# Grouped attention with split values and the probabilities of four query blocks in one matmul

## The chip, the cores and the metric

One core of one Trainium2 chip runs one program. The time is the device time of one execution in microseconds (us), the median of several. The engines are TensorE (PE; its weight loads are listed as PEld), VectorE (DVE), ScalarE (ACT), GpSimd (POOL) and SyncE (SP), which issues the DMAs.

## The reference, cut to what matters

The program is a chain of two transformer blocks. The change touches one stage of the second: attention of 512 latent tokens, 8 query heads in 2 groups, over 768 keys (512 latent and 256 context ones), without a mask.

```python
q, k, v = jnp.split(h @ w_qkv, [nq, nq + nk], axis=-1)    # 8 q heads, 2 k, 2 v, width 128
q = _rmsnorm(q..., q_gain); k = _rmsnorm(k..., k_gain)    # and rotary on the latent ones
keys = jnp.concatenate([kl, kc], axis=1)                  # 768
s = jnp.einsum('bqkgd,bskd->bkgqs', q, k).astype(jnp.float32) * (ATTN_HEAD_DIM ** -0.5)
p = jax.nn.softmax(s, axis=-1).astype(v.dtype)
o = jnp.einsum('bkgqs,bskd->bqkgd', p, v)
y_lat = o @ w_o
```

All is float32. The kernel forms nearly all products from two parts (`hi`, the rounded value in the format fp32r, and `lo`, the rest): `three()` makes one product of three fp32r matmuls, hi by hi, hi by lo and lo by hi.

## The kernel before

Every engine has its own program, written out by hand, and the engines wait for each other through counting semaphores; what stands behind a waiting instruction on its engine waits too.

Projection. `project(g, ...)` runs for g = 0 to 3: keys and values of the context, keys and values of the latents, queries 0 to 3, queries 4 to 7. Each g is four chunks of weights (`b + 4g` to `b + 4g + 3`) and uses the four PSUM banks `4 * (g % 2)` and up, so g = 2 writes over the banks of g = 0, and g = 3 over those of g = 1. The weights go through four slots: ACT makes `w_hi` (`split_hi`, L1909) once a slot is free, DVE then makes `w_lo` (`split_lo`, L1929). Values are turned by PE from `vT_att` into banks 2 and 3 (g = 0) or 4 and 5 (g = 1) in `value_turns`, and ACT copies them to `v_att` (L2303, semaphore `vt_s`). PE waits for that copy (`vt_s`) before `project(2)` and `project(3)`.

Attention. A unit is a head u; it has four query blocks c of 128 tokens. A step is (u, c), 32 steps in all. In a step PE turns the 6 x 128 probabilities of the block (`turn_`, L1124, two groups of three), makes the scores of the block two steps later (`scores`, three fp32r matmuls of 512 and three of 256 columns, L1045 to L1047), and multiplies the turned probabilities with the values (`values`, L1135): 6 matmuls of plain f32 with 128 columns, each listed as two records. DVE takes the scores out with scale and maximum (`maxima`, L2699), ACT makes the exponentials (`exps`, L2018), and the turned probabilities leave PSUM half on DVE (`take`, L2709), half on ACT (L2026). `finish` (L2715, L2725) divides by the sum on DVE, with queries on partitions.

Output. `project_out` first turns the eight head outputs (32 transposes, L1254), ACT and DVE split them (L2100, L2843), and then `three()` multiplies them with the chunks of `attn_w_o`.

The last queries are prepared between the scores of the first two blocks and the first `turn_` (`last_queries`, handed in as `beside`).

Of the kernel before, what the change touches and what calls it, by code (L numbers as in the profile page):

```python
# [28 lines left out]
P = 128  # L29
# [152 lines left out]
def build(nc, w, tables, out):  # L182
    ctx = ExitStack()
    with ctx:
# [96 lines left out]
        class Work:  # L281


            def __init__(self, tag, at, size, start, width):
                self.sm = arena("scores" + tag, [P, 2, width], F32, at, size, start)
                self.pT = arena("probs_T" + tag, [P, 2, 512], F32, at + 8 * width, size, start)

# [28 lines left out]
        v_att = arena("v_att", [P, 6, 2 * P], F32, 22528)  # L316
        vT_att = arena("vT_att", [P, 2, SEQ], F32, 28672)
        o_att = arena("o_att", [P, 4, D_MODEL], F32, 32768)
        zeros = arena("zeros", [P, SEQ + CTX], F32, 49152)

        work_att = Work("_att", 52224, ARENA_SIZE, None, 3072)
# [95 lines left out]
        rl_s = sem("rl_s")  # L417
        spread_s = sem("spread_s")
# [132 lines left out]
        def attention_plan(heads, blocks, **what):  # L551

            full = blocks == "full"
            units = len(heads)
            at = Phase("attention", units=units, heads=heads, full=full, per_t=8 if full else 4, **what)
            at.tab_in = tab_s.planned
            at.s0, at.sm0 = s_s.plan(4 * units), sm_s.plan(4 * units)
            at.p0, at.t0, at.ptd0, at.pta0 = p_s.plan(4 * units), t_s.plan(at.per_t * units), ptd_s.plan(at.per_t // 2 * units), pta_s.plan(at.per_t // 2 * units)
            at.pv0, at.o0, at.step0 = pv_s.plan(at.per_t * units), o_s.plan(units), dve_step.plan(sum(3 if h["gate"] is not None else 1 for h in heads))
            return at  # L560
# [36 lines left out]
        def out_plan(ph, tile, turned):  # L597

            ph.o_tile = tile
            if turned:  # L600
                ph.tr0 = tr_s.plan(KT)
            ph.oh0, ph.ol0 = a_hi_s.plan(KT), a_lo_s.plan(KT)
            ph.d0 = down_s.plan(KT - 1)
            x_done.plan(KT)
            bank_half[0] ^= 4

        def even_phase():
# [37 lines left out]
            out_plan(ph, o_tile, False)  # L645
            return ph

        def mla_phase():
# [22 lines left out]
            out_plan(ph, o_tile, False)  # L671
# [24 lines left out]
        def attn_phase():  # L696
# [14 lines left out]
            for i in range(2):  # L711
                splits.append((k_att[:, i, :], k_att_hi[:, i, :], k_att_lo[:, i, :]))
                for u in range(4):
                    h = 4 * i + u
                    splits.append((q_att[:, h, :], q_att_hi[:, h, :], q_att_lo[:, h, :]))
                    heads.append(dict(q=splits[-1][1:], k=splits[5 * i][1:], v=lambda kb, i=i: v_att[:, kb, i * P:i * P + P],
                                      out=o_att[:, :, h * P:h * P + P], gate=None, need=ph.qk0 + len(splits),
                                      scale=lambda c, h=h: q_rstd[:, 4 * h + c:4 * h + c + 1]))
            ph.first_splits = splits[0:4]
            ph.att = attention_plan(heads, "full", work=work_att, mask=zeros[:, :], dim=P, later=[[x] for x in splits[4:]])  # L720
            ph.att.nrm0, ph.att.rstd_in = ph.nrm0, ph.head_rstd0 + 6
            out_plan(ph, lambda k: (a_hi[:, k, :], a_lo[:, k, :]), True)
# [317 lines left out]
        def _(pe):  # L1040
# [46 lines left out]
            def attention(at, beside=None):  # L1087

                wk, full, per_t, D = at.work, at.full, at.per_t, at.dim
                ring = 2 if full else 4  # L1090
                units_t = [(c, range(3 * h, 3 * h + 3)) for c in range(4) for h in range(2)] if full else \
                    [(c, range(c + 1)) for c in range(4)]

                def scores(u, c):
                    head = at.heads[u]
                    if c == 0 and head["need"] is not None:
                        pe.wait_ge(qk_lo_s.sem, head["need"])
                    if c == 0 and head.get("rope") is not None:
                        pe.wait_ge(rope_in[4].sem, 16 * 4)
                        pe.wait_ge(head["rope"].sem, 16 * 4)  # L1100
                    if 4 * u + c >= ring:

                        pe.wait_ge(sm_s.sem, at.sm0 + 4 * u + c - ring + 1)
                    parts = [(0, 512, 2 * (c % 2)), (512, 768, 2 * (c % 2) + 1)] if full else [(0, (c + 1) * P, c)]
# [2507 lines left out]
```

## Time and profile before

| | us |
|---|---|
| median of 3 runs | 3199.8 (3199.59 to 3200.89) |
| the profiled execution | 3202.26 |
| its span, first to last instruction | 3200.4 |
| PE busy in the span | 3131.4 (98%) |
| stretch from the first `turn_` to the first output matmul | 2675.86 to 2778.51 |

The execution's time is 1.86 us more than its span. Positions in the trace are given in us from the span's start.

### The profile page before, as it was taken

Reading aid. Unit: us, or ns where it says so; the run is one execution under the profiler, and the core shown is the slowest. Engines: PE = TensorE matmul, PEld = TensorE weight load, DVE = VectorE, ACT = ScalarE, POOL = GpSimd, SP = SyncE. Lnnn points to the kernel's source line nnn. Section 1 sums busy time; section 2 is a strip of 40 time slices with the busy share of each in tenths; the row PEclk is TensorE's granted clock in tenths of the full one; section 3 lists DMA queues with packets and bytes.
Section 4 is the critical chain, followed back from the end, with each engine's and each line's share of the span. In section 5 each row is a group of like instructions: output and inputs, shape, how many; then the busy total and the mean of one; then the engine's idle time right before and its main releaser. Section 6 shows DMA issues by size and latency. Waiting matters only on the chain.

```text
span 3200.4 us, 43004 instructions
## 1 busy us (share of the span) xinstructions
PE 3131.4 (98%) x15821; PEld 2601.3 (81%) x15821; DVE 1969.8 (62%) x2773; ACT 1258.4 (39%) x1920; POOL 177.8 (6%) x176
## 2 busy tenths in 40 slices
PE   8999999899999999999999999999999999999999
PEld 6888877678888888886788888989888887878887
DVE  6764557866755676457765554897555465565543
ACT  3222323752222422236642233765334354453332
POOL 1000011100000000000120000332000001000000
PEclk9999999999999999999999999999999999999999
DMA  6543342025532454332145433554332220123332
GB/s 182 169 139 102 107 123 66 1 78 159 164 116 94 126 169 145 99 98 66 52 137 168 135 102 106 165 153 144 92 104 93 91 98 7 33 73 97 100 100 71
DMA packets 388599, 346.11 MB, mean 108 GB/s; under 512 B 12512, under 2 KB 340637, under 8 KB 388477
## 3 DMA queue, kind: packets, MB, share of 16 engines
q1 hardware_dynamic: 388477, 344.49, 35.8%
q8 instruction: 76, 1.25, 0.2%
q14 instruction: 46, 0.38, 0.0%
HBM read 338.22 MB, written 2.10 MB: 106 GB/s over the span
## 4 chain that ended last, share of the span: by engine, by line
PE 87%; DVE 8%; ACT 3%; issue 1%; SPq 1%; DMA 0%; POOL 0%; ACTq 0%; DVEq 0%; POOLq 0%
PE ps L1045 26%; PE ps L1047 26%; PE ps L1046 26%; DVE w_lo L1929 2%; PE ps L1135 1%; ACT scores_even L2061 1%; PE ps L1193 1%; PE ps L1208 1%; PE ps L1228 1%; SPq L936 1%; PE ps L1124 1%; DVE scores_even L2773 0%; PE ps L1787 0%; PE ps L1788 0%; PE ps L1786 0%
## 5 line engine op out<-in xcount | busy, mean ns | idle before, releaser
L1045 PE MATMUL ps<-a_hi,w_hi 128*128 128x512 f32 (+1 forms) x2920 | 1106.0, 379 | 23.7 <-DVE w_lo L1929 8.4
L1046 PE MATMUL ps<-a_lo,w_hi 128*128 128x512 f32 (+1 forms) x2920 | 1098.9, 376 | 0.0
L1047 PE MATMUL ps<-a_hi,w_lo 128*128 128x512 f32 (+1 forms) x2920 | 1098.4, 376 | 0.0
L1929 DVE TENSOR_TENSOR w_lo<-w_raw,w_hi 128x1024 fp32r<-128x1024 f32 (+1 forms) x526 | 642.1, 1244 | 178.9 <-ACT w_hi L1909 176.1
L1909 ACT ACTIVATE w_hi<-w_raw 128x1024 fp32r<-128x1024 f32 (+1 forms) x526 | 543.6, 1046 | 362.6 <-PE ps L1047 302.4
L1045 PEld LDWEIGHTS ps<-a_hi,w_hi 128*128 128x128 f32 x2920 | 551.9, 189 | 129.1 <-issue 20.4
L1046 PEld LDWEIGHTS ps<-a_lo,w_hi 128*128 128x128 f32 x2920 | 552.2, 189 | 101.1 <-issue 2.0
L1047 PEld LDWEIGHTS ps<-a_hi,w_lo 128*128 128x128 f32 x2920 | 551.9, 189 | 100.6
L1045 PE MATMUL ps<-hs_hi,w_hi 128*128 128x512 f32 x1008 | 392.7, 390 | 1.0 <-DVE hs_lo L3274 1.0
L1047 PE MATMUL ps<-hs_hi,w_lo 128*128 128x512 f32 x1008 | 392.2, 389 | 0.0
L1046 PE MATMUL ps<-hs_lo,w_hi 128*128 128x512 f32 x1008 | 392.2, 389 | 0.0
L2396 ACT ACTIVATE t<-t 128x512 f32<-128x512 f32 x88 | 55.6, 632 | 518.9 <-DVE t L3251 518.9
L3253 DVE TENSOR_TENSOR t<-ps,rstd 128x512 f32<-128x512 f32 x88 | 60.8, 691 | 293.8 <-PE ps L1047 293.8
L2410 ACT ACTIVATE hs_hi<-hid 128x512 fp32r (+1 forms) x126 | 79.5, 631 | 406.0 <-PE ps L1047 406.0
L1045 PEld LDWEIGHTS ps<-hs_hi,w_hi 128*128 128x128 f32 x1008 | 189.2, 188 | 40.7 <-DVE hs_lo L3274 1.5
L1047 PEld LDWEIGHTS ps<-hs_hi,w_lo 128*128 128x128 f32 x1008 | 189.2, 188 | 39.2
L1046 PEld LDWEIGHTS ps<-hs_lo,w_hi 128*128 128x128 f32 x1008 | 189.2, 188 | 39.1
L3274 DVE TENSOR_TENSOR hs_lo<-hid,hs_hi 128x512 fp32r<-128x512 f32 x106 | 73.3, 691 | 218.2 <-ACT hs_hi L2410 218.2
L3239 DVE SCALAR_TENSOR_TENSOR t<-ps,cols,t 128x511 f32<-128x511 f32 x88 | 66.0, 750 | 188.0 <-ACT t L2389 187.9
L3296 DVE SCALAR_TENSOR_TENSOR ada_acc<-ada_raw,cond,ada_acc 128x1024 f32<-128x1024 f32 x147 | 180.5, 1279 | 0.0
L2389 ACT ACTIVATE t<-ps,cols 128x512 f32<-128x512 f32 x88 | 68.6, 779 | 206.5 <-PE ps L1047 206.5
L3266 DVE TENSOR_TENSOR hid<-t,t 128x512 f32 x108 | 74.8, 693 | 17.9 <-DVE t L3253 9.6
(394 smaller groups left out, 3105.2 us busy)
## 6 DMA issues: line engine op xcount, KB each, us to landing
w_raw<-in_ffn_w_up SPq DMA_DIRECT2D x220, 512.0 KB, 4.7
w_raw<-in_ffn_w_down SPq DMA_DIRECT2D x154, 512.0 KB, 3.5
ada_raw<-in_ada_w SPq DMA_DIRECT2D x96, 512.0 KB, 3.9
w_raw<-in_ffn_w_gate SPq DMA_DIRECT2D x88, 512.0 KB, 4.9
w_raw<-in_ev_w_in SPq DMA_DIRECT2D x20, 512.0 KB, 4.4
w_raw<-in_attn_w_qkv SPq DMA_DIRECT2D x12, 512.0 KB, 3.9
w_raw<-in_mla_w_out SPq DMA_DIRECT2D x8, 512.0 KB, 3.6
w_raw<-in_attn_w_o SPq DMA_DIRECT2D x8, 512.0 KB, 3.5
```

The source lines that it names most:

```text
L1045: mm(dst, hi, rhi, start=start, stop=False)
L1046: mm(dst, hi, rlo, start=False, stop=False)
L1047: return mm(dst, lo, rhi, start=False, stop=stop)
L1909: nc.scalar.activation(w_hi[:, s, 0:width], w_raw[:, s, 0:width], ACT.Copy).then_inc(hi_made.sem, 1)
L1929: nc.vector.tensor_tensor(w_lo[:, s, 0:width], w_raw[:, s, 0:width], w_hi[:, s, 0:width].bitcast(F32), ALU.subtract).then_inc(lo_made.sem, 1)
L2389: do(t[:, 0:T], ps[:, ph.half + 2 * (f % 2) + side, 0:T], ACT.Identity, scale=conv_column(1, side, f, it), bias=conv_column(3, side, f, it ...
L2410: do(dst, src, ACT.Copy).then_inc(h_hi_s.sem, 1)
L3239: v.scalar_tensor_tensor(t[:, 1:T], src[:, 0:T - 1], conv_column(0, side, f, it), t[:, 1:T], ALU.mult, ALU.add).then_inc(mid.sem, 1)
L3253: v.tensor_tensor(t2[:, 0:T], ps[:, f2 + 1, 0:T], rstd[:, 0:T], ALU.mult).then_inc(up_s.sem, 1)
L3266: v.tensor_tensor(hid[:, bass.ds(it * 2 + f, 1), 0:T], t1[:, 0:T].unsqueeze(1), t2[:, 0:T].unsqueeze(1), ALU.mult).then_inc(h_s.sem, 1)
L3274: v.tensor_tensor(lo, src, hi.bitcast(F32), ALU.subtract).then_inc(h_lo_s.sem, 1)
L3296: last = v.scalar_tensor_tensor(acc, ada_raw[:, u, :], cond[:, c, bass.ds(it, 1)], acc, ALU.mult, ALU.add)
```

## The change

Values are kept in two parts, `v_att_hi` (ACT) and `v_att_lo` (DVE, new `value_rests`), and PE waits for the second part (`vl_s`) before `project(2)` and `project(3)`. In attention the values are the stationary operand. For each of the six key blocks j of a head, PE turns the probabilities of all four query blocks into one bank (four transposes), ACT rounds them to `pT_att_hi`, DVE makes `pT_att_lo` after that, and `three()` adds v x p with 512 columns. The head's output then has its features on partitions. The inverses of the sums are spread over partitions by four more transposes (`inverse_rows`), ACT takes them to `o_att`, DVE multiplies (`scaled`), ACT and DVE split the result (`out_hi`, `out_lo`) into the places where the head's queries lay. `project_out` has no transposes any more, and takes the output columns in the order 4 to 7, 0 to 3 for its first chunk.

```diff
-                    pe.wait_ge(vt_s.sem, ph.vt0 + 2)
+                    pe.wait_ge(vl_s.sem, ph.vl0 + 2)
...
-                    pe.wait_ge(vt_s.sem, ph.vt0 + 4)
+                    pe.wait_ge(vl_s.sem, ph.vl0 + 4)
...
-                    for i, kb in enumerate(kbs):
-                        last = mm(ps[:, 6 + u % 2, c * D:(c + 1) * D], wk.pT[:, j % 2, i * P:(i + 1) * P],
-                                  at.heads[u]["v"](kb), start=(kb == 0), stop=(kb == (5 if full else c)))
-                    last.then_inc(pv_s.sem, 1)
...
+                    slot = (6 * u + j) % 2
+                    three(ps[:, 6 + u % 2, :], *at.heads[u]["v"](j), pT_att_hi[:, slot, :], pT_att_lo[:, slot, :], j == 0, j == 5)\
+                        .then_inc(pv_s.sem, 1)
+
+                scores(0, 0)
+                scores(0, 1)
+                beside()
+                scores(0, 2)
+                scores(0, 3)
                 for u in range(at.units):
...
+                    for j in range(7):
+                        if j < 6:
+                            turn_(u, j)
+                        else:
+                            inverse_rows(u)
+                        if j < 4 and u + 1 < at.units:
+                            scores(u + 1, j)
+                        if j:
+                            values(u, j - 1)
...
+                for c in range(4):
                     exps(0, c)
                 for u in range(at.units):
...
+                    for j in range(6):
+                        turned_hi(u, j)
+                        if 1 <= j <= 4 and u + 1 < at.units:
                             exps(u + 1, j - 1)
...
+                        if j == 2 and u:
+                            out_hi(u - 1)
+                        if j == 4 and u < len(at.later):
+                            if u != 1:
+                                act.wait_ge(nrm_s.sem, at.nrm0 + 6 + max(0, u - 1))
+                            qk_hi(at.later[u])
+                    rows_taken(u)
+                out_hi(at.units - 1)
...
+                def turned_lo(u, j):
+                    n = 6 * u + j
+                    dve.wait_ge(pta_s.sem, at.pta0 + 7 * u + j + 1)
+                    v.tensor_tensor(pT_att_lo[:, n % 2, :], ps[:, 4 + (7 * u + j) % 2, :], pT_att_hi[:, n % 2, :].bitcast(F32),
+                                    ALU.subtract).then_inc(ptd_s.sem, 1)
...
+                    inverse(u)
+                    for j in range(6):
+                        turned_lo(u, j)
+                        if j < 4 and u + 1 < at.units:
                             maxima(u + 1, j)
...
+                        if j == 1 and u:
+                            scaled(u - 1)
+                        if j == 2 and u < 4:
+                            roped(u)
+                        if j == 3 and u:
+                            out_lo(u - 1)
+                        if j == 5 and u < len(at.later):
+                            qk_lo(at.later[u], split0 + u)
...
                     split_lo(dve, b + 6)
                     split_lo(dve, b + 7)
+                    value_rests(0, 2)
                     values(1)
...
                     split_lo(dve, b + 10)
+                    value_rests(1, 4)
                     split_lo(dve, b + 11)
```

DVE in the projection, from the weights `b + 6` and `b + 7` on, of the changed kernel (the lines of its own source):

```order
L1910 TENSOR_TENSOR w_lo<-w_raw,w_hi 128x1024 [waits hi_made] x2
L3037 TENSOR_TENSOR v_att_lo<-ps,v_att_hi 128x2x128 [waits vt_s] x2
L3029 COPY vT_att<-ps 128x512 [waits tv_s,w_used]
L3029 COPY vT_att<-ps 128x512 [waits tv_s]
L1910 TENSOR_TENSOR w_lo<-w_raw,w_hi 128x1024 [waits hi_made] x2
```

The row with `v_att_lo` is new; the others stand as before. A second such row (128x4x128, x2) stands between the `w_lo` of `b + 10` and that of `b + 11`.

PE in attention before, one step (the semaphore `p_s` is ACT's exponentials, `ptd_s` and `pta_s` are the turned probabilities taken by DVE and ACT, `sm_s` the scores taken):

```order
L1124 MATMUL ps<-ident,scores_att 128x128 [waits ptd_s,p_s]
L1124 MATMUL ps<-ident,scores_att 128x128 x2
L1124 MATMUL ps<-ident,scores_att 128x128 [waits pta_s,p_s]
L1124 MATMUL ps<-ident,scores_att 128x128 x2
L1045 MATMUL ps<-k_att_hi,q_att_hi 128x512 [waits sm_s]
L1046 MATMUL ps<-k_att_lo,q_att_hi 128x512
L1047 MATMUL ps<-k_att_hi,q_att_lo 128x512
L1045 MATMUL ps<-k_att_hi,q_att_hi 128x256
L1046 MATMUL ps<-k_att_lo,q_att_hi 128x256
L1047 MATMUL ps<-k_att_hi,q_att_lo 128x256
L1135 MATMUL ps<-v_att,probs_T_att 128x128 [waits ptd_s]
```

PE in attention of the changed kernel, the last part of a head, from the values of j = 3 on (`stats` holds the inverses of the sums, `rl_s` says that they are made):

```order
L1043 MATMUL ps<-pT_att_hi,v_att_hi 128x512 [waits ptd_s]
L1044 MATMUL ps<-pT_att_lo,v_att_hi 128x512
L1045 MATMUL ps<-pT_att_hi,v_att_lo 128x512
L1118 MATMUL ps<-ident,scores_att 128x128 [waits ptd_s]
L1118 MATMUL ps<-ident,scores_att 128x128 x3
L1043 MATMUL ps<-pT_att_hi,v_att_hi 128x512 [waits ptd_s]
L1044 MATMUL ps<-pT_att_lo,v_att_hi 128x512
L1045 MATMUL ps<-pT_att_hi,v_att_lo 128x512
L1290 MATMUL ps<-ident,stats 128x128 [waits ptd_s,rl_s]
L1290 MATMUL ps<-ident,stats 128x128 x3
L1043 MATMUL ps<-pT_att_hi,v_att_hi 128x512 [waits ptd_s]
```

Before, each step held 1.13 us of scores between `turn_` and `values`. Now the scores of the next head go with j = 0 to 3, and j = 4, j = 5 and the inverses have none between turning and multiplying.

## Rows read from the trace of the kernel before

**Rows 1.** The page, part 1: busy us, share and instructions of each engine.

```profile
PE 3131.4 (98%) x15821; PEld 2601.3 (81%) x15821; DVE 1969.8 (62%) x2773; ACT 1258.4 (39%) x1920; POOL 177.8 (6%) x176
```

**Rows 2.** Windows of the attention stage: length, busy us (instructions) by engine, clock, DMA.

```profile
2675.80:2773.40 97.60, 96.22 (x756) 91.27 (x756) 61.68 (x120) 46.94 (x98) 0.98 (x1) 1.00 0.01 1
```

**Rows 3.** Timeline of PE, one step: start, us from first start to last end.

```profile
2698.13 0.82 PE L1124 MATMUL ps<-ident,scores_att 128*128 128x128 f32 x6
2698.71 0.48 PE L1045 MATMUL ps<-k_att_hi,q_att_hi 128*128 128x512 f32 x1
2699.03 0.39 PE L1046 MATMUL ps<-k_att_lo,q_att_hi 128*128 128x512 f32 x1
...
2699.72 0.28 PE L1047 MATMUL ps<-k_att_hi,q_att_lo 128*128 128x256 f32 x1
2699.84 1.50 PE L1135 MATMUL ps<-v_att,probs_T_att 128*128 128x128 f32 x12
...
2701.17 0.82 PE L1124 MATMUL ps<-ident,scores_att 128*128 128x128 f32 x6
```

**Rows 4.** Timeline of DVE and ACT in the same step.

```profile
2700.04 1.02 DVE L2699 CUSTOM_DVE_ANT_0 scores_att<-ps,zeros,q_rstd 128x768 f32<-128x768 f32 x1 [0.68 <-PE ps L1047]
2700.98 0.08 DVE L2699 DVE_READ_ACCUMULATOR2_ANT stats<- 128x1 f32 x1
...
2701.10 0.94 ACT L2018 ACTIVATE scores_att<-scores_att,stats 128x768 f32<-128x768 f32 x1 [1.62 <-DVE stats L2699]
...
2701.94 0.19 ACT L2018 ACTIVATION_READ_ACCUMULATOR scores_att<-scores_att,stats 128x1 f32 x1
2702.04 0.48 ACT L2026 ACTIVATE probs_T_att<-ps 128x384 f32<-128x384 f32 x1
```

**Rows 5.** Groups by line and form: busy us, mean ns, idle before.

```profile
L2100 ACT ACTIVATE a_hi<-ps 128x512 fp32r<-128x512 f32 x8 | 4.5, 601 | 3.0 <-PE ps L1254 2.9
L2604 DVE TENSOR_TENSOR a_lo<-t,a_hi 128x256 fp32r<-128x256 f32 x16 | 6.7, 419 | 0.0
```

**Rows 6.** Timeline, all engines, from the last values to the output.

```profile
2771.78 1.60 PE L1135 MATMUL ps<-v_att,probs_T_att 128*128 128x128 f32 x12 [0.32 <-DVE probs_T_att L2709]
2773.49 0.69 DVE L2725 TENSOR_TENSOR o_att<-ps,stats 128x512 f32<-128x512 f32 x1 [1.68 <-PE ps L1135]
...
2774.24 4.52 PE L1254 MATMUL ps<-ident,o_att 128*128 128x128 f32 x32 [0.85 <-DVE o_att L2725]
...
2775.56 4.28 DVE L2843 TENSOR_TENSOR a_lo<-ps,a_hi 128x512 fp32r<-128x512 f32 x7 [1.38 <-ACT a_hi L2100]
...
2778.51 0.47 PE L1045 MATMUL ps<-a_hi,w_hi 128*128 128x512 f32 x1
```

**Rows 7.** Timeline around the first `turn_`.

```profile
2675.72 2.20 DVE L2675 TENSOR_TENSOR q_att_lo<-q_att,q_att_hi 128x512 fp32r<-128x512 f32 x2
...
2675.86 0.88 PE L1124 MATMUL ps<-ident,scores_att 128*128 128x128 f32 x6 [0.78 <-DVE vT_att L3063]
...
2677.85 0.54 DVE L2709 COPY probs_T_att<-ps 128x384 f32<-128x384 f32 x1
...
2678.45 0.38 PE L1135 MATMUL ps<-v_att,probs_T_att 128*128 128x128 f32 x1 [0.66 <-DVE probs_T_att L2709]
```

**Rows 8.** Timeline around the start of `project(2)`, at 2601.78.

```profile
2601.10 0.39 PE L1045 MATMUL ps<-a_hi,w_hi 128*128 128x512 f32 x1
...
2601.78 0.39 PE L1045 MATMUL ps<-a_hi,w_hi 128*128 128x512 f32 x1
...
2602.04 1.06 ACT L1909 ACTIVATE w_hi<-w_raw 128x1024 fp32r<-128x1024 f32 x1 [4.38 <-PE ps L1047]
...
2603.13 1.23 DVE L1929 TENSOR_TENSOR w_lo<-w_raw,w_hi 128x1024 fp32r<-128x1024 f32 x1 [4.21 <-ACT w_hi L1909]
...
2604.27 1.28 DVE L3079 COPY vT_att<-ps 128x512 f32<-128x512 f32 x2
```

**Rows 9.** Timeline around the start of `project(3)`, at 2627.88.

```profile
2627.14 1.22 DVE L1929 TENSOR_TENSOR w_lo<-w_raw,w_hi 128x1024 fp32r<-128x1024 f32 x1
...
2627.88 0.39 PE L1045 MATMUL ps<-a_hi,w_hi 128*128 128x512 f32 x1
```

**Rows 10.** Windows around falls of the clock, and around two idle stretches of PE.

```profile
2643.00:2647.00 4.00, 4.00 (x7) 1.72 (x6) 1.75 (x3) 0.00 (x0) 2.85 (x3) 0.57 0.26 103
2658.60:2661.30 2.70, 0.01 (x1) 0.04 (x1) 1.56 (x2) 2.60 (x5) 0.00 (x0) 1.00 0.01 3
2822.30:2824.50 2.20, 0.00 (x0) 0.00 (x0) 2.07 (x4) 1.46 (x3) 0.00 (x0) 0.96 0.00 0
2824.00:2835.00 11.00, 6.79 (x22) 5.58 (x23) 6.32 (x11) 7.12 (x11) 0.00 (x0) 0.53 0.01 1
```

More of the change, by code:

```diff
@@ L1085, in late_turns, with attention, bank @@
                     to_features(ctx_tok, 2, k, 5 + turn % 3)
[L1087 to L1092, printed above, removed]
+            def attention(at, beside):
+                def bank(u, j):
+                    return 4 + (7 * u + j) % 2
@@ L1094, in scores @@
                 def scores(u, c):
                     head = at.heads[u]
-                    if c == 0 and head["need"] is not None:
+                    if c == 0:
                         pe.wait_ge(qk_lo_s.sem, head["need"])
[L1098 to L1103, printed above, removed]
@@ L1113, in scores @@
-                    last.then_inc(s_s.sem, 1)
+                    if 4 * u + c >= 2:
+                        pe.wait_ge(sm_s.sem, at.sm0 + 4 * u + c - 1)
+                    q = [t[:, c * P:(c + 1) * P] for t in head["q"]]
+                    for first, end, to in ((0, 512, 2 * (c % 2)), (512, 768, 2 * (c % 2) + 1)):
+                        k = [t[:, first:end] for t in head["k"]]
+                        last = three(ps[:, to, 0:end - first], q[0], q[1], k[0], k[1], True, True)
+                    last.then_inc(s_s.sem, 1)
@@ L1137, in values @@
-                    last.then_inc(pv_s.sem, 1)
-                if full:
-                    steps = [(u, c) for u in range(at.units) for c in range(4)]
-                    scores(0, 0)
-                    scores(0, 1)
-                    if beside is not None:
-                        beside()
-                    for t, (u, c) in enumerate(steps):
-                        turn_(u, 2 * c)
-                        turn_(u, 2 * c + 1)
-                        if t + 2 < len(steps):
-                            scores(*steps[t + 2])
-                        values(u, 2 * c)
-                        values(u, 2 * c + 1)
-                    return
@@ L2009, in attention @@
             def attention(at):
-                wk, full, per_t = at.work, at.full, at.per_t
                 MX, L = stats[:, 0:2, :], stats[:, 4:6, :]
@@ L2097, in split_out @@
             def split_out(ph, n0):
-                for k in range(KT) if ph.kind == "attn" else ():
-                    act.wait_ge(tr_s.sem, ph.tr0 + k + 1)
-                    do(ph.o_tile(k)[0], ps[:, ph.half + k % 4, :], ACT.Copy).then_inc(a_hi_s.sem, 1)
                 for k in range(KT):
```

267 lines of the change are left out of this document (100 added, 167 removed).

## The prediction

> **What bounds the kernel now.** I read the page first: PE is busy for 98% of the span and DVE for 62% [rows 1], so time is won or lost only where PE works less, waits less or waits more. Then the window of the attention stage: of 97.60 us PE is busy 96.22 at full clock, DVE 61.68, ACT 46.94 [rows 2]. The reader is to see that PE hardly waits there, that the other two have slack, and that DMA does nothing. The timeline gives the period: PE starts to turn at 2698.13 and again at 2701.17, so a step is 3.04 us and a head of four steps 12.16 [rows 3]. Within a step turning lasts to 2698.71 (0.58 us for six transposes, 0.097 each), scores to 2699.84 (1.13), values to 2701.17 (1.33, so 0.222 for each f32 matmul of 128 columns). These are distances from start to start, which is what a PE that never waits pays; the durations in the rows overlap.
>
> The profiled execution took 3202.26 us, 2.5 above the median of 3199.8. My sum is a difference between two traces, and I add it to the median.
>
> **Prices.** PE: an fp32r matmul of 512 columns costs 0.228 (three from 2601.10 to 2601.78 [rows 8]); the first after transposes costs 0.32 (2698.71 to 2699.03 [rows 3]), 0.09 more. Leaving a wait costs PE another 0.1: the last values, after a wait, take 1.60 instead of 1.50 [rows 3, 6]. From one engine to the next: DVE starts on the scores at 2700.04, and the last matmul, begun at 2699.72 and 0.28 long, ended at 2700.00; maxima end at 2701.06, ACT starts at 2701.10 [rows 3, 4]. So a hop costs some 0.04, and 0.07 where PE's transposes are left; back to PE it costs 0.06 to 0.12 (0.06 from 2677.85 + 0.54 to 2678.45 [rows 7]). Maxima: 1.02 to its end, 0.94 to DVE's next instruction. Exponentials with their sum: 1.03 to the end (2701.10 to 2701.94 + 0.19), 0.94 to ACT's next [rows 4]. Rounding 512 columns out of PSUM on ACT: 0.60 [rows 5], and with the same overlap of 0.08 as the neighbours in [rows 4], 0.52 to the next. The rest on DVE: 0.69, and 0.60 to the next ((4.28 - 0.69) / 6 [rows 6]). None of the added instructions is of another kind than these.
>
> **Term 1, PE's own work, a gain.** Per head now: 24 transposes for the probabilities and 4 for the inverses, 28 x 0.097 = 2.71; four score blocks, unchanged, 4 x 1.13 = 4.50; six `three()` of values, 18 x 0.228 = 4.10; and 0.09 three more times, for the values that follow transposes directly. Together 11.58, against 12.16: 0.58 less per head. The values themselves fall from 24 x 0.222 = 5.32 to 4.10; the added transposes and changes of format take back half of that.
>
> **Term 2, the start, a loss.** Before, PE turned block 0 as soon as `last_queries` was over, at 2675.86 [rows 7]. Now the first turning takes all four query blocks, so it waits for all four exponentials, and only two are made. PE does scores 2 and 3 first, 2675.86 to 2678.03. DVE is busy with the rests of the queries until 2677.85 [rows 7], then maxima 2 and 3: start 2677.85 and 2678.79, end 2679.81. ACT: exponentials of block 3 from 2679.85 to 2680.88. PE turns at 2680.94, 5.08 after 2675.86. PE waits 2.9 of it.
>
> **Term 3, waits at the end of each head, a loss.** A product needs a chain through two engines: PE turns, ACT rounds, DVE takes the rest, PE multiplies. Count from the start of turning j = 4. PE: turn 4 from 0, values 3 from 0.39, turn 5 from 1.16, and at 1.55 it wants values 4. ACT can round at 0.29 + 0.27 + 0.07 = 0.63 (last transpose begun, its 0.27, the hop) and ends at 1.23; DVE takes the rest from 1.27 to 1.96; PE goes on at 2.02. Wait: 0.47. Then values 4 to 2.9, inverses to 3.28, and PE wants values 5. On ACT, behind rounding 4 (next instruction at 1.15) stand the exponentials of block 3 of the next head (0.94) and the rounding of a later query (0.52), and only then rounding 5, from 2.61 to 3.21, though turn 5 was done at 1.8. DVE's rest 5 then ends at 3.94, PE goes on at 4.0. Wait: 0.72. With 0.1 for each way out of a wait a head loses 1.39. The second head rounds keys (128x768) there and loses 0.2 more; the seventh has no query to round and loses 0.87. For j = 0 to 3 the scores (1.13) lie between turning and multiplying and cover the chain: I walked the three lists through a head, and PE waits there nowhere. The new DVE load is no bound: four maxima 3.76, six rests 3.6, the scaled output, its rest, a rotation, a later query and the inverse some 2.8, 10.2 in all under 12.97. The eighth head has no scores beside it. Its PE work is 7 x 0.39 + 6 x 0.77 = 7.35 and its waits 1.24 before the first values and 0.47 before every second one, with exits 2.5.
>
> **Term 4, the output, a gain.** Between the last values' start plus 1.60 (2773.38) and the first output matmul at 2778.51 lie 5.13 us: the last division, 32 transposes, splits [rows 6]. All of it goes. The first output columns go to banks 0 to 3, so the last head's scaling and split hide behind 2.7 us of matmuls. The weights are already split for two chunks, as before.
>
> **Attention as a whole.** Before: 2675.86 to 2778.51, 102.65 us [rows 6, 7]. After: 5.08 + 7 x 11.58 + 7.35 + waits (5 x 1.39 + 1.6 + 0.87 + 2.5) = 105.4. **A loss of 2.8.**
>
> **Term 5, the rests of the values, a loss.** This lies ahead of attention and is bigger. PE waited for ACT's copy of the context's values before `project(2)`, and never stood still there. Now it waits for `v_att_lo`, which DVE makes only after `w_lo` of chunk `b + 7`. That chunk uses the slot of `b + 3`, which PE gives back with the end of `project(1)`: ACT starts `w_hi` at 2602.04, released by PE, DVE `w_lo` at 2603.13, and its next instruction starts at 2604.27 [rows 8]. The two rests of 256 columns (0.42 each [rows 5], 0.34 apart) therefore end at 2605.03, PE starts at 2605.15 instead of 2601.78: **3.37 lost**. Chance plays no part in it: the wait at the start of `project(2)` depends on the end of `project(1)` through two engines. Queued behind PE's wait is everything; behind the new DVE work stand the copies of `vT_att`, not wanted before 2621. The second pair stands behind `w_lo` of `b + 10`, which begins at 2627.14 at the end of DVE's chain on the keys, itself released by PE's matmuls in `project(2)` and so shifted with it. Next start 1.14 later, at 2628.28; two rests of 512 columns, 0.60 + 0.69, end at 2629.57; PE starts at 2629.70 instead of 2627.88 [rows 9]: **1.82 lost**. Nothing later gives this back: `w_lo` of `b + 11`, pushed by 1.2, is wanted three blocks of 5.4 us later, and where PE waits for `k_att_hi` at 2658.6, that wait begins with PE's own last matmul.
>
> **Term 6, the clock, a loss.** PE's granted clock has two levels, 1.2 and 2.4 GHz. After 2.2 us without a matmul it fell (mean 0.53 from 2824 to 2835); after 2.7 us at 2658.6 it did not; from 2643 to 2647 it had a mean of 0.57, which is 4 x 0.43 = 1.7 us of full-speed work lost [rows 10]. The new idle stretch of 3.4 us at 2601.8 is longer than both. I take one fall of the small kind: **1.7 lost**. The bounds are 0 (as at 2658.6) and, with falls also at the start of attention (2.9 idle) and in the eighth head, three times 1.7 = 5.1. The Trainium skill ("TensorE: Matmul & The Clock Gate", section "Why this matters for your kernels") warns that an idle gap between bursts of matmuls brings the clock back to its half level. [...]
>
> **The sum.** 3.37 + 1.82 + 2.8 + 1.7 = 9.7; 3199.8 + 9.7 = 3209.5. A measurement of this kernel can tell 0.2%, 6.4 us, from no change.
>
> **Rivals.**
> (a) Forecast: both waits of term 5 and the waits of term 3, with one fall: 3209.5; with none 3207.8.
> (b) The clock falls two times more: 3213. For it: the 2.2 us gap that sufficed. Against: the 2.7 us that did not.
> (c) Not slower: the chain through ACT and DVE does not hold PE up in attention. Place: values 4 and 5 of each head. If rounding and rest were ready in time, all the waits there, 11.9 us, would go: attention 93.5, a gain of 9.1, and with term 5 and one fall 3199.8 - 9.1 + 6.9 = 3197.6. It decides from where the chain takes less than the 1.55 us of PE's cover instead of 2.0. For it: a chain with shorter hops. Against: 0.60 and 0.69 are means of eight equal instructions.
> (d) The rests cost PE nothing, if ACT's slot were free earlier: 3199.8 + 2.8 = 3202.6. Against: the release by PE is in the row.
> The Trainium skill has a rule that would make the matmuls cheaper (same page, section "Back-to-back issue gap": sustained 131 ns for 512 columns, where the row has 228). By it the values of a head would take 18 x 0.131 = 2.4 us; PE would only wait longer, since the chain of term 3 sets the pace there. The row decides.
>
> **How the numbers follow.** Chances: (a) 0.57, (b) 0.2, (c) 0.09, (d) 0.06, and 0.08 for something between (a) and (d), with part of a wait hidden. The range has 3203 as its lower end (between (d) and (a)) and 3214.5 as its upper end: (b) with 1.5 more for errors of the walk, in which some thirty small waits are added up. Faster by over 0.2% (under 3193.4) needs (c) and (d) together: 0.03. Slower by over 0.2% (over 3206.2): nearly all of (a) and (b), 0.76. The rest is 0.21.
>
> **What would show it.** Term 5: PE idle before the first matmul of `project(2)`, released by DVE's `v_att_lo`, 3.3 us, and before `project(3)`, 1.8 us. Term 2: PE idle 2.9 before the first turning. Term 3: a head every 12.97 us, with two waits on `pT_att_lo` per head, 0.5 and 0.7. Term 1: values at 0.23 per matmul. Term 4: output matmuls right behind the last values. Term 6: a stretch at half clock after 2605. I am wrong if a head takes under 12.2, or if PE starts `project(2)` without a wait.

## The result, and the profile after

| | before | after |
|---|---|---|
| median, us | 3201.28 (8 runs, 3199.59 to 3208.27) | 3211.87 (8 runs, 3210.61 to 3214.6) |
| ratio | | 1.0028, 95% interval 1.0019 to 1.0037 |
| profiled execution, us | 3202.26 | 3211.78 (span 3210.0) |

The change makes the kernel 10.6 us (0.3%) slower. The forecast was 3209.5, 9.7 slower. The two profiled executions differ by 9.52 us.

The page's first part, to be laid beside [rows 1]: PE is busy for 2.0 us less (3131.4 - 3129.4) in a span that is 9.6 longer, so the span grows by waiting. The busy time itself holds some microseconds at the lower clock, which are counted below.

```profile
PE 3129.4 (97%) x15581; PEld 2586.1 (81%) x15581; DVE 1983.5 (62%) x2793; ACT 1275.4 (40%) x1944; POOL 177.8 (6%) x176
```

The timeline at the start of `project(2)`, beside [rows 8]. The order is the one that the prediction named: ACT's `w_hi`, DVE's `w_lo`, then the two rests as one row, then PE.

```profile
2600.62 0.39 PE L1045 MATMUL ps<-a_hi,w_lo 128*128 128x512 f32 x1
2601.11 1.06 ACT L1890 ACTIVATE w_hi<-w_raw 128x1024 fp32r<-128x1024 f32 x1 [4.38 <-PE ps L1045]
...
2602.20 1.23 DVE L1910 TENSOR_TENSOR w_lo<-w_raw,w_hi 128x1024 fp32r<-128x1024 f32 x1 [4.21 <-ACT w_hi L1890]
...
2603.34 0.75 DVE L3037 TENSOR_TENSOR v_att_lo<-ps,v_att_hi 128x256 fp32r<-128x256 f32 x2
...
2604.19 0.47 PE L1043 MATMUL ps<-a_hi,w_hi 128*128 128x512 f32 x1 [3.18 <-issue]
```

PE would have gone on at 2600.85 (2600.62 and the 0.23 of a matmul) and goes on at 2604.19: 3.34 lost. The bracket's 3.18 is less, since it counts from the modelled end of the matmul before, and it names no releaser, though `v_att_lo` ends at 2604.09; that the rests hold PE there is shown by the experiments that move them. The same at the start of `project(3)`, beside [rows 9]: 2632.02 would have been, 2633.79 is, 1.77 lost.

```profile
2631.79 0.39 PE L1045 MATMUL ps<-a_hi,w_lo 128*128 128x512 f32 x1
...
2632.41 1.28 DVE L3037 TENSOR_TENSOR v_att_lo<-ps,v_att_hi 128x512 fp32r<-128x512 f32 x2
...
2633.79 0.47 PE L1043 MATMUL ps<-a_hi,w_hi 128*128 128x512 f32 x1 [1.61 <-issue]
```

The start of attention, beside [rows 7]: 5.09 us from the scores of block 2 to the first turning. The scores behind it then come at half speed (2688.38 to 2690.44 for one block, 2.06 where 1.14 is normal).

```profile
2682.52 0.50 PE L1043 MATMUL ps<-k_att_hi,q_att_hi 128*128 128x512 f32 x1 [0.79 <-DVE vT_att L3013]
...
2687.61 1.11 PE L1118 MATMUL ps<-ident,scores_att 128*128 128x128 f32 x4 [2.74 <-ACT scores_att L1997]
2688.38 0.78 PE L1043 MATMUL ps<-k_att_hi,q_att_hi 128*128 128x512 f32 x1
...
2690.44 0.77 PE L1118 MATMUL ps<-ident,scores_att 128*128 128x128 f32 x4
```

The end of a head (there is nothing like it in [rows 3, 4]): from turning j = 4 at 2748.57 to values 4 at 2750.59, and from turning j = 5 at 2749.71 to values 5 at 2752.50. ACT rounds j = 5 at 2751.14, behind an exponential and a later query.

```profile
2748.57 0.60 PE L1118 MATMUL ps<-ident,scores_att 128*128 128x128 f32 x4
...
2749.21 0.60 ACT L2005 ACTIVATE pT_att_hi<-ps 128x512 fp32r<-128x512 f32 x1 [0.69 <-PE ps L1118]
...
2749.71 0.60 PE L1118 MATMUL ps<-ident,scores_att 128*128 128x128 f32 x4
2749.84 0.69 DVE L2674 TENSOR_TENSOR pT_att_lo<-ps,pT_att_hi 128x512 fp32r<-128x512 f32 x1
...
2750.59 0.50 PE L1043 MATMUL ps<-pT_att_hi,v_att_hi 128*128 128x512 f32 x1 [0.28 <-DVE pT_att_lo L2674]
2750.62 0.62 ACT L1988 ACTIVATE q_att_hi<-q_att 128x512 fp32r<-128x512 f32 x1
...
2751.14 0.59 ACT L2005 ACTIVATE pT_att_hi<-ps 128x512 fp32r<-128x512 f32 x1
...
2752.50 0.50 PE L1043 MATMUL ps<-pT_att_hi,v_att_hi 128*128 128x512 f32 x1 [0.52 <-DVE pT_att_lo L2674]
```

PE's waits in this stage by releaser (us in total, times, longest): sixteen on the rest, one on the exponentials.

```profile
PE ps L1043 <- DVE pT_att_lo L2674: 6.8, 16, 1.0
PE ps L1118 <- ACT scores_att L1997: 2.7, 1, 2.7
```

The output, beside [rows 6]: it follows 0.23 behind the last values.

```profile
2787.75 0.39 PE L1045 MATMUL ps<-pT_att_hi,v_att_lo 128*128 128x512 f32 x1
2787.98 0.40 PE L1043 MATMUL ps<-q_att_hi,w_hi 128*128 128x512 f32 x1
```

Windows of stretches with a low clock (length, PE, PEld, DVE, ACT and POOL busy, granted clock, DMA), beside [rows 10]: behind the new gap; the part wholly at half clock ahead of attention; from the first scores to the start of attention; behind the first turning. In the first, 5.40 x (1 - 0.68) / 0.5 is 3.5 us at half clock.

```profile
2604.00:2609.40 5.40, 5.21 (x16) 4.19 (x17) 1.28 (x3) 0.30 (x1) 0.00 (x0) 0.68 0.31 97
2666.90:2680.50 13.60, 13.53 (x45) 10.24 (x44) 3.44 (x6) 6.30 (x12) 2.31 (x2) 0.50 0.00 0
2665.62:2682.52 16.90, 16.04 (x52) 11.58 (x52) 5.03 (x10) 7.58 (x14) 4.11 (x4) 0.60 0.00 0
2687.00:2691.00 4.00, 3.39 (x15) 3.10 (x15) 1.19 (x3) 1.16 (x3) 0.00 (x0) 0.57 0.01 4
```

The stretch of 16.90 holds the same work in the kernel before, where it takes 2.33 less at a clock of 0.77, with 6.9 us at half clock (7.50 x 0.46 / 0.5) in place of 13.6:

```profile
2661.29:2675.86 14.57, 12.94 (x52) 8.57 (x53) 4.94 (x10) 7.58 (x14) 4.12 (x4) 0.77 0.00 0
2666.90:2674.40 7.50, 7.50 (x19) 4.25 (x19) 1.55 (x3) 4.54 (x8) 2.66 (x3) 0.54 0.00 0
```

So the 9.52 us of the two traces are: -0.93 ahead of `project(2)` (nothing there is changed), 3.34 and 1.77 of waits, 1.73 in `project(2)` (27.83 from 2604.19 to 2632.02, where the clock falls behind the gap, against 26.10), -1.58 from the start of `project(3)` to the first scores (31.83 against 33.41, where the fall of before at 2643 is missing), 2.33 of a longer stretch at half clock, 2.81 in attention (105.46, from 2682.52 to 2787.98, against 102.65) and 0.05 behind it. The -0.93 is for the most part the clock too: before has falls at 1619 and 2026 that the changed kernel's trace lacks, and lacks the one that this has at 1496 (windows of the kernel before, and then of the changed one):

```profile
1490.00:1505.00 15.00, 11.90 (x60) 7.78 (x60) 13.35 (x45) 11.48 (x32) 0.00 (x0) 1.00 0.30 95
2022.00:2035.00 13.00, 12.05 (x91) 12.00 (x91) 11.19 (x18) 8.41 (x14) 1.58 (x2) 0.87 0.64 182
```

```profile
1490.00:1505.00 15.00, 12.56 (x52) 7.91 (x50) 12.80 (x42) 11.33 (x31) 0.00 (x0) 0.89 0.29 91
2022.00:2035.00 13.00, 12.04 (x103) 11.99 (x102) 12.08 (x19) 9.28 (x14) 2.02 (x2) 1.00 0.62 181
```

### The profile page after: what moved, and what is told of

Same layout as the page of the kernel before. It is cut to its first block, busy times and chain, and to the rows that moved or that the text cites. A ratio compares the mean times of both kernels' runs of the same rounds, so it can differ in the third digit from the quotient of the medians.

```text
span 3210.0 us, 42515 instructions
## 1 busy us (share of the span) xinstructions
PE 3129.4 (97%) x15581; PEld 2586.1 (81%) x15581; DVE 1983.5 (62%) x2793; ACT 1275.4 (40%) x1944; POOL 177.8 (6%) x176
## 4 chain that ended last, share of the span: by engine, by line
PE 86%; DVE 8%; ACT 3%; issue 2%; SPq 1%; DMA 0%; POOL 0%; ACTq 0%; DVEq 0%; POOLq 0%
PE ps L1043 26%; PE ps L1044 26%; PE ps L1045 26%; DVE w_lo L1910 2%; PE ps L1176 1%; ACT scores_even L2045 1%; PE ps L1191 1%; PE ps L1211 1%; SPq L934 1%; PE ps L1118 1%; DVE scores_even L2727 0%; PE ps L1769 0%; PE ps L1768 0%; PE ps L1767 0%; DVE scores_even L2748 0%
## 5 line engine op out<-in xcount | busy, mean ns | idle before, releaser
L1043 PE MATMUL ps<-a_hi,w_hi 128*128 128x512 f32 (+1 forms) x2856 | 1080.7, 378 | 29.6 <-DVE w_lo L1910 9.5
L1045 PE MATMUL ps<-a_hi,w_lo 128*128 128x512 f32 (+1 forms) x2856 | 1073.9, 376 | 0.0
L1044 PE MATMUL ps<-a_lo,w_hi 128*128 128x512 f32 (+1 forms) x2856 | 1073.9, 376 | 0.0
L1043 PEld LDWEIGHTS ps<-a_hi,w_hi 128*128 128x128 f32 x2856 | 539.5, 189 | 134.2 <-issue 26.1
L1044 PEld LDWEIGHTS ps<-a_lo,w_hi 128*128 128x128 f32 x2856 | 539.7, 189 | 98.3 <-issue 1.7
L1045 PEld LDWEIGHTS ps<-a_hi,w_lo 128*128 128x128 f32 x2856 | 539.4, 189 | 98.1
L3227 DVE TENSOR_TENSOR hid<-t,t 128x512 f32 x108 | 74.8, 693 | 17.9 <-DVE t L3214 9.6
```

The costliest lines, as they stand in the source:

```text
L1043: mm(dst, hi, rhi, start=start, stop=False)
L1044: mm(dst, hi, rlo, start=False, stop=False)
L1045: return mm(dst, lo, rhi, start=False, stop=stop)
L3227: v.tensor_tensor(hid[:, bass.ds(it * 2 + f, 1), 0:T], t1[:, 0:T].unsqueeze(1), t2[:, 0:T].unsqueeze(1), ALU.mult).then_inc(h_s.sem, 1)
```

## The experiments

Each comparison is with the kernel before on the same chip, 3201.99 (31 runs) for the rests early, both roundings first, the scores spread and the layout without the rests, and 3201.89 (33 runs) for the others. The changed kernel stands 10.6 above before, in its own comparison. The intervals of the ratios are some 3 us to either side, so below 3 us the traces have to tell.

**The rests of the values early.** DVE makes them before the `w_lo` that wait for a slot.

```diff
+                    value_rests(0, 2)
                     split_lo(dve, b + 6)
                     split_lo(dve, b + 7)
-                    value_rests(0, 2)
...
                         key_roped(i)
+                        if i == 1:
+                            value_rests(1, 4)
                         key_normed(1, i)
                     split_lo(dve, b + 10)
-                    value_rests(1, 4)
```

> The changed kernel, with DVE making the rests of the context's values before w_lo of b + 6, and those of the latents' values ahead of the second key's norm. My theory (term 5: PE stands still before project(2) and project(3) only because the rests are queued behind w_lo): both waits go, 3.3 and 1.9 us of the changed trace, and with the long gap the fall of the clock after 2605, 1.7; the stretch from the end of project(1) to the start of attention goes from 81.7 to 75 us, the time from 3211.9 to 3205. Rival: the rests cost PE nothing and the loss is all in attention: the time stays at 3211.9 within 1.

Measured: 3205.58, ratio 1.001 (1.0 to 1.002), 3.6 above before and so 7.0 below the changed kernel. From the end of `project(1)` to the start of attention it takes 74.78 us (2601.71 to 2676.49), as expected. Both waits are gone, and in the window 2602 to 2612, where the changed kernel had its half clock, it is full:

```profile
2602.00:2612.00 10.00, 10.00 (x46) 8.29 (x45) 3.65 (x4) 4.22 (x6) 0.00 (x0) 1.00 0.30 83
2659.52:2676.49 16.97, 15.99 (x52) 11.52 (x52) 5.03 (x10) 7.57 (x14) 4.10 (x4) 0.60 0.00 0
```

The second row is the stretch from the first scores to attention; it is as long as in the changed kernel, with no gap in the projection. So the long stretch at half clock doesn't need the waits in the projection. Attention stays at 105.47 us (2676.49 to 2781.96).

**The first rests early alone.**

```diff
+                    value_rests(0, 2)
                     split_lo(dve, b + 6)
                     split_lo(dve, b + 7)
-                    value_rests(0, 2)
```

> Only the first pair of rests (context values, before project(2)) is moved ahead of the weights that wait for a slot; the second pair stays where the change has it. Theory (the gap of 3.2 us brings the half clock at 2605): no wait and no fall of the clock there, 3.3 + 1.7 = 5.0 us less than the changed kernel; the wait of 1.6 before project(3) stays: before + 5. Rival (the clock falls there for another reason, or falls elsewhere instead): 3.3 us less, before + 6.7.

Measured: 3207.91, ratio 1.0019 (1.0009 to 1.0028), 6.0 above before, between the two expectations and not told apart by the medians. The trace has a full clock from 2600 to 2610, and the wait of 1.61 before `project(3)`:

```profile
2600.00:2610.00 10.00, 10.00 (x46) 8.28 (x45) 3.65 (x4) 3.59 (x6) 0.00 (x0) 1.00 0.33 100
2662.13:2676.70 14.57, 12.95 (x52) 8.57 (x52) 4.93 (x10) 7.58 (x14) 4.12 (x4) 0.77 0.00 0
```

The second row, the same stretch as above, is here as short as in the kernel before. But from 2640.82 to 2647.65 PE has a granted clock of 0.50, 6.8 us where the kernel before has 3.4 at the same work: a fall came elsewhere, as the rival allowed. So the run shows that the fall behind the gap goes with the gap, and not that its 1.7 us are saved.

**The rests alone, in the kernel before.** Attention and output are those of before; nobody reads the rests.

```diff
-                    pe.wait_ge(vt_s.sem, ph.vt0 + 2)
+                    pe.wait_ge(vl_s.sem, ph.vl0 + 2)
...
-                    pe.wait_ge(vt_s.sem, ph.vt0 + 4)
+                    pe.wait_ge(vl_s.sem, ph.vl0 + 4)
...
                     split_lo(dve, b + 6)
                     split_lo(dve, b + 7)
+                    value_rests(0, 2)
...
                     split_lo(dve, b + 10)
+                    value_rests(1, 4)
```

> The kernel before, with the rests of the values alone: DVE makes them at the places where the changed kernel does, PE waits for them before project(2) and project(3), nobody reads them, and attention is that of before. Theory: 3.2 to 3.4 us idle before project(2), 1.6 to 1.8 before project(3), and one fall of the clock of 3.4 us at half speed behind the first: before + 6.7. Rival (the gap does not bring the fall): before + 5. Second rival (the waits are cover for other waits in the projection, so part comes back): before + 3.

Measured: 3208.37, ratio 1.002 (1.0011 to 1.0029), 6.5 above before: more than half of the change's whole loss, from two waits far from the part that it rewrites. The last matmul of `project(1)` starts at 2600.64, the next at 2604.21, which is 3.34 of wait again (2600.64 + 0.23 to 2604.21), and the clock falls behind it. The interval, 3.5 to 9.3 us, excludes that the rests cost nothing; it can't tell 6.7 from 5 or 3.

```profile
2604.20:2609.40 5.20, 5.19 (x16) 4.12 (x17) 1.10 (x2) 0.11 (x1) 0.00 (x0) 0.67 0.33 101
```

**Both roundings first.** ACT rounds j = 5 ahead of the exponentials and the later query of j = 4.

```diff
                     for j in range(6):
-                        turned_hi(u, j)
+                        if j < 5:
+                            turned_hi(u, j)
+                        if j == 4:
+                            turned_hi(u, 5)
```

> The changed kernel, with ACT rounding the turned probabilities of j = 5 right after those of j = 4, ahead of the next head's exponentials. My theory (term 3: the 0.7 us wait at values 5 comes from what is queued on ACT, the 0.5 us at values 4 from the length of the chain through ACT and DVE): the wait at values 5 goes or falls to 0.3, the one at values 4 stays at 0.3 to 0.5; a head takes 12.2 to 12.5 us instead of 13.0, attention 101.5 instead of 105.5, the time 3208. Rival: both waits are the chain's length, the order on ACT is nothing: a head stays at 13.0.

Measured: 3208.14, ratio 1.0016 (1.0007 to 1.0026), 6.2 above before. The wait at values 5 is gone, that at values 4 stays, a head takes 12.0 to 12.3 us where it took 12.3 to 13.0, and attention 101.29 (2686.38 to 2787.67). In the timeline ACT rounds j = 5 at 2751.30, and values 5 follow the inverses after 0.36:

```profile
2751.30 0.60 ACT L2005 ACTIVATE pT_att_hi<-ps 128x512 fp32r<-128x512 f32 x1 [0.53 <-PE ps L1118]
2751.55 0.50 PE L1043 MATMUL ps<-pT_att_hi,v_att_hi 128*128 128x512 f32 x1 [0.28 <-DVE pT_att_lo L2677]
...
2752.35 0.60 PE L1290 MATMUL ps<-ident,stats 128*128 128x128 f32 x4
...
2752.71 0.47 PE L1043 MATMUL ps<-pT_att_hi,v_att_hi 128*128 128x512 f32 x1
```

**The scores spread.** The scores of the next head go with j = 0, 1, 2 and 4, so that turning j = 4 has cover; maxima and exponentials move with them.

```diff
-                        if j < 4 and u + 1 < at.units:
-                            scores(u + 1, j)
+                        if j in (0, 1, 2, 4) and u + 1 < at.units:
+                            scores(u + 1, min(j, 3))
...
-                        if 1 <= j <= 4 and u + 1 < at.units:
-                            exps(u + 1, j - 1)
+                        if j in (1, 2, 3, 5) and u + 1 < at.units:
+                            exps(u + 1, (0, 0, 1, 2, 0, 3)[j])
```

> The changed kernel, with the fourth block of the next head's scores moved from j = 3 to j = 4 (and its maximum and exponentials with it, the exponentials behind the rounding of j = 5). My theory (the waits stand where no scores cover the chain): only one wait of 0.5 us is left in a head, at values 5; a head takes 12.15 us, as before the change; attention 100.0 us, the time 3206.5. Rival: the cover is short at any place, and a wait of the same size comes up at the bare step j = 3: 13.0 us as now.

Measured: 3204.39, ratio 1.0007 (0.9998 to 1.0017), 2.4 above before. A head takes 12.0, with one wait:

```profile
2736.72 0.60 PE L1290 MATMUL ps<-ident,stats 128*128 128x128 f32 x4
2737.61 0.50 PE L1043 MATMUL ps<-pT_att_hi,v_att_hi 128*128 128x512 f32 x1 [0.29 <-DVE pT_att_lo L2674]
```

Attention takes 100.31 (2683.76 to 2784.07). The wait at values 5 is 0.53 here (2736.72 + 0.36 to 2737.61). The rest of a head, 11.5, is PE's own work. The expected time was 3206.5, 2.1 too high.

**The layout without the rests.** Values and turned probabilities in plain f32, one matmul of 512 columns for each j, no `pT_att_lo`, no `v_att_lo`; turning, inverses and output as changed. It computes the same product in the other format.

```diff
-                    three(ps[:, 6 + u % 2, :], *at.heads[u]["v"](j), pT_att_hi[:, slot, :], pT_att_lo[:, slot, :], j == 0, j == 5)\
+                    mm(ps[:, 6 + u % 2, :], at.heads[u]["v"](j)[0], pT_att_hi[:, slot, :], start=(j == 0), stop=(j == 5))\
...
-                        turned_lo(u, j)
```

> One part of the change alone: values stand in the array and the turned probabilities of four blocks stream past, but values and probabilities are not split (one plain f32 matmul of 512 columns instead of three fp32r ones, ACT alone copies the turned probabilities, no rests, PE waits for ACT's copy of the values as before the change). My theory: without the rests no wait in the projection and none in a head; PE's own work is 2.7 turning, 4.5 scores, 5.2 to 5.3 values, 12.5 us a head; attention 5.1 + 7 x 12.5 + 8.2 = 100.8, 1.9 less than before the change; the time 3199.5 where before has 3201.3. Rival: plain f32 with 512 columns is dearer than with 128, or ACT alone can't keep pace: a head above 13 us, the time at 3204 or more.

Measured: 3204.4, ratio 1.0007 (0.9997 to 1.0017), 2.4 above before. Attention took 103.72 (2677.67 to 2781.39), 2.9 more than my estimate: a head takes 12.7, and values in f32 0.86 from their start to the next turning, against 0.69 for `three()`:

```profile
2743.76 0.60 PE L1114 MATMUL ps<-ident,scores_att 128*128 128x128 f32 x4
2744.20 1.02 PE L1128 MATMUL ps<-pT_att_hi,v_att_hi 128*128 128x512 f32 x2
2745.06 0.60 PE L1114 MATMUL ps<-ident,scores_att 128*128 128x128 f32 x4
```

Nor was it faster: the expectation (3199.5, 1.8 below before) was missed. The rival names the wrong cause. The matmuls cost what I had counted, 0.86 for each j, where four of 128 columns were 4 x 0.222 = 0.89; and a head stays under 13. What I had left out is that with no scores between them the values start 0.43 us after the turning (2745.06 to 2745.49) and 0.61 after the inverses (2746.35 to 2746.96), where scores start 0.35 after it (2741.41 to 2741.76), and that behind the inverses they take 0.97: that is most of the 0.2 us a head over my 12.5. The other 1.6 us are the first head (14.35), which has the half clock behind the wait before it, as in the changed kernel. This run also separates two parts of the change: the layout alone costs PE 0.54 us a head (12.70 against 12.16), and only the product in parts makes it cheaper than before.

**The start early.** Scores and maxima of blocks 2 and 3 of the first head ahead of the last queries.

```diff
-                beside()
                 scores(0, 2)
                 scores(0, 3)
+                beside()
...
-                beside()
                 maxima(0, 2)
                 maxima(0, 3)
+                beside()
```

> Scores and maxima of query blocks 2 and 3 of the first head are put ahead of the last queries, all else is the changed kernel. Theory (the wait of 2.7 us before the first turning comes from two exponentials that are made only after the last queries): the first turning starts without a wait of over 0.3 us, and the kernel is 2.9 to 3.7 us faster than the changed one (the scores, 2.2 us, move ahead of the last queries, partly into an idle time of PE of 0.8 us there): before + 6 to + 7 us. The heads stay at 12.8 us with their two waits. Rival (DVE's rests of the queries, not the exponentials, hold up PE there): the wait moves to the last queries and nothing is won, before + 10.

Measured: 3205.16, ratio 1.001 (1.0001 to 1.0019), 3.3 above before: 7.3 below the changed kernel, twice the 2.9 to 3.7 expected. The wait was not gone either:

```profile
2680.71 0.92 ACT L1997 ACTIVATE scores_att<-scores_att,stats 128x768 f32<-128x768 f32 x1
...
2681.87 0.63 PE L1118 MATMUL ps<-ident,scores_att 128*128 128x128 f32 x4 [1.35 <-ACT scores_att L1997]
```

ACT makes all four exponentials behind the last queries in its own list, which I left as it was; I had overlooked that. From the first scores to the first turning it is 14.98 (2666.89 to 2681.87), against 21.99 in the changed kernel (2665.62 to 2687.61). But the two don't have the same clock there: this trace has 3.4 us at half clock (below), the changed kernel's 13.6. The difference of 10.2 us costs 3.5, if it costs what it did between the changed kernel and before (2.33 for 6.8), and 5.1 if all of it counts by half. By this estimate the edit itself is worth 1.9 to 3.5 us of the 7.0, and not twice what I expected. The second row is the work behind the first turning, where the wait of 1.35 has a fall behind it:

```profile
2676.12:2679.54 3.42, 3.42 (x6) 1.34 (x5) 1.38 (x2) 3.39 (x5) 2.54 (x2) 0.50 0.00 0
2682.90:2686.40 3.50, 3.50 (x12) 3.12 (x13) 2.17 (x5) 0.69 (x2) 0.00 (x0) 0.51 0.00 0
```

**All three together.** The edits of the rests early, the scores spread and the start early, as above; their first lines:

```diff
+                    value_rests(0, 2)
                     split_lo(dve, b + 6)
...
+                        if j in (0, 1, 2, 4) and u + 1 < at.units:
+                            scores(u + 1, min(j, 3))
...
                 scores(0, 2)
                 scores(0, 3)
+                beside()
```

> Three edits together: the rests of the values ahead of the weights that wait for a slot, the scores of the next head with j = 0, 1, 2 and 4 of the present one in place of 0 to 3, and the early scores of the first head. Theory (the three losses are separate and add): 6.3 us back in the projection with the fall of the clock, as measured alone; 5.2 in the heads (stretch 105.4 to 100.3, as measured alone), 3.3 at the start, 14.8 in all, so about 5 us faster than the kernel before: before - 5, between - 7 and - 2. PE waits at most once a head, 0.3 us. Rival (the fall of the clock and the waits share time, so that the gains overlap): before - 1 to + 2.

Measured: 3194.66 (11 runs, 3191.06 to 3197.17), ratio 0.9977 (0.9968 to 0.9986): 7.2 faster than before, a little outside the - 7 to - 2 expected, and 17.8 below the changed kernel. The three edits alone were 7.0, 8.2 and 7.3 below it, 22.5 together, so they overlap in part, though the sum is still more than the 14.8 expected. The two traces differ by 17.2: 3.9 up to the first scores (2665.62 against 2661.74), 7.0 from there to the first turning (21.99 against 14.97) and 6.3 from there to the output (100.37 against 94.03). Part of that is clock: 3.4 us at half clock ahead of the first turning where the changed kernel has 13.6, and none behind it. The gain over before is hardly clock: over all executions the mean granted clock is 0.9909 here and 0.9906 before, which makes up about 1 us of the 7.2, with an error of 1.5. No execution of it was as slow as the fastest of before (3199.25). From the first turning to the output it takes 94.03 (2676.71 to 2770.74) at full clock, and its waits on the rest sum to 3.6 us (window, and group by line with the idle time at its end):

```profile
2676.70:2770.80 94.10, 90.40 (x537) 75.43 (x538) 74.80 (x138) 65.19 (x125) 0.17 (x1) 1.00 0.00 1
```

```profile
L1043 PE MATMUL ps<-pT_att_hi,v_att_hi 128*128 128x512 f32 x48 | 21.5, 448 | 3.6 <-DVE pT_att_lo L2674 3.6
```

## Why the prediction was right, and where it was not

**Term 1, PE's own work.** Right. A head of the kernel with spread scores takes 12.0 with 0.5 of waiting, so 11.5 where 11.58 was worked out and 12.16 was before. The change does save work, though by the product in parts and not by the layout, which alone took 12.7; in the changed kernel the saving is hidden behind the waits.

**Term 2, the start.** Right: 5.09 for 5.08, PE idle 2.74 for 2.9.

**Term 3, the waits of a head.** Right in mechanism and place, a little too large. The chain from turning to values 4 took 2.02 as worked out (2748.57 to 2750.59), that from turning j = 5 to values 5 2.79 for 2.84. A head took 12.8 and not 12.97, since I added 0.1 for leaving a wait on top of the 0.09 that a first matmul behind transposes costs; the rows have 0.33 for it with a wait (2750.59 to 2750.92) and 0.32 without [rows 3]. Rival (c) needed a chain that holds nothing up. With one delay on ACT removed (both roundings first) five heads became 0.5 to 1.0 shorter, and with cover (scores spread) 0.75 to 1.0: it holds PE.

**Term 4, the output.** Right, the output matmuls follow directly.

**Term 5, the rests of the values.** Right: 3.34 and 1.77 for 3.37 and 1.82, and the rests alone, put into the kernel before, cost 6.5 with the clock. Rival (d), that they cost nothing, is out.

**Term 6, the clock.** The mechanism was right; that one fall fits the total is luck. The fall behind the new gap came as forecast, in all five traces that have this gap (the changed kernel, the rests alone, both roundings first, scores spread, start early), and in none of the five without it. But in the changed kernel's trace the fall of before at 2643 [rows 10] was missing, so that these two cancel; the fall at the start of attention, which I had given to rival (b), came and cost 1.5 (the first head is that much longer than the others: 0.42 in the first turning, 0.92 in the scores, 0.18 in the second turning); and the stretch of one-column matmuls before attention ran 2.33 longer. From `project(2)` on the clock thus cost 4.0 (1.73 - 1.58 + 2.33 + 1.5), with the 0.93 gained ahead of it 3.1, and not 1.7. The shorter heads (1.5) make up for the difference.

The step that was wrong is the count of falls. The fall at the start of attention isn't a matter of chance: the half clock begins within 0.4 us of the first turning in all six traces that wait 2.5 to 2.7 us before it (granted clock 0.50 to 0.55 in the 3.4 us from the first turning on), and neither of the two that turn without such a wait with the old attention has it (1.00). With a wait of 1.35 one of two has it. So the change brings two falls and not one. Against that stand falls that come and go without an edit; and [rows 10] left out the half clock of before from 2667.3 to 2674.1, so the forecast put what happens to it at nothing. The third fall of rival (b), in the eighth head, didn't come.

All executions together are a better measure than one trace. Their mean granted clock is 0.9905 and 0.9906 for the kernel before (31 and 33 runs) and 0.9899 for the changed one (8 runs). If all of that fell on work that PE is waited for, it is some 2 us more lost to the clock (3210 x 0.0101 less 3200 x 0.0095), with an error of about 1: the 1.7 are not excluded. All six kernels with the long wait before the first turning have a mean of 0.9890 to 0.9900; the rests alone has 0.9903, the start early and all three together 0.9909. Attention's 105.46 for 105.4 hides an exchange: 1.5 less in the heads, 1.5 more for the fall.

The Trainium skill ("TensorE: Matmul & The Clock Gate", section "Why this matters for your kernels") warns of idle gaps between bursts of matmuls. The traces agree for the gap of 3.18 us, and show the fall behind the wait of 2.5 to 2.7 before the first turning too. Directly behind the gap of 1.6 before `project(3)` none of the six traces that have it shows a fall.

In absolute terms the forecast is 2.4 low: 1.5 since the kernel before had a median of 3201.28 in the comparison and not 3199.8, 0.9 in the difference.

**What stays open.** Why the stretch from the first scores to attention takes 14.57 us at times and 16.9 to 17.0 at others. Traces with the short form: before, the rests alone, the first rests early; with the long one: changed, rests early, scores spread (2666.78 to 2683.76); both roundings first and the layout without rests took 17.9 and 18.0. The last queries and PE's order in it are the same, and no edit of mine goes with it. With one trace for each kernel I can't say whether it is chance from execution to execution; the 2.3 us are less than the 8 us over which the executions of before spread, and that spread goes with the clock (0.993 in those of 3199.6 to 3199.8, 0.988 in those of 3205.9 and 3207.6). Against pure chance speaks that five of the six kernels with the long wait before attention have the long form and neither of the two with the old attention; no run decides it.

## What to carry to other kernels

A value that becomes two parts has a second producer, and that producer has a list. Look where the new instruction stands in it and what is in front: here two subtractions of 0.4 us cost 3.3 us of PE time, because a weight waited in front of them for a slot that PE itself gives back. Moving them up two lines returned it.

A cheaper product with a longer chain through other engines wins only where PE has other work between turning and multiplying. Count the chain (2.02 us here) against the cover of every step, above all at the ends of loops, and spread the filling work (here four score blocks over seven steps) so that the uncovered steps are few. The change itself lost 10.6 us; with three reorderings, and the same arithmetic, it won 7.2. Part of those 17.8 us is a better clock, as said above.

Where engines' lists are separate, an edit of two lists is not an edit of the third: the exponentials stayed behind and left 1.35 us of waiting.

A trace with another pattern of half clock doesn't measure an edit by itself. Look at the granted clock of both stretches before laying a difference to the edit, as with the start early.

## What the runs showed of the hardware

The granted clock fell for stretches of different lengths: 3.4 us behind the gap, 6.9 us in the kernel before and 13.6 us in the changed one in the same work. A fall of 3.4 us behind the gap cost 1.73 us. Behind 3.18 us without a matmul it fell in five of five traces, behind 2.5 to 2.7 us before the first turning in six of six, directly behind 1.6 us in none of six. Behind the same wait of 2.70 us before the first scores, the half clock began 1.3 us after PE went on in the changed kernel and 6 us after it in the kernel before (2661.29 to 2667.3).

A plain f32 matmul of 512 columns took 0.86 us from its start to the next instruction (listed as two records, 0.43 each), three fp32r matmuls with the same columns 0.69. The product in parts was cheaper on PE than the one in plain f32.
